# The order of gather and adding transfers in a mixture-of-experts loop

## The reference, cut to what matters

```python
logits = hf @ w_router + b_router
top_vals, top_idx = lax.top_k(logits, 4)
top_w = softmax(top_vals)
# for every block of rows that go to one expert e:
    xb  = hf[tok]                                              # gather
    hid = clamped_swiglu(xb @ w_gate_up[e] + b_gate_up[e])     # 1024 -> 2048 -> 1024
    out = (hid @ w_down[e] + b_down[e]) * wt[:, None]          # 1024 -> 1024
y = segment_sum(outs, row_tok)                                 # adding, four rows per token
x = rms_norm(x + gate2 * y)
```

## Time and profile before

| | |
|---|---|
| median of three runs | 2173.54 us |
| the profiled execution | 2171.81 us |
| its span | 2170.0 us |
| TensorE busy in the span | 2047.2 us, 94% |
| VectorE, ScalarE, GpSimd busy | 837.4, 264.7, 279.2 us |
| moved by DMA | 546.12 MB |
| TensorE matmuls of `gate_up` | 6336, which is 33 items of 192 |
| gathers | 34 |
| adding transfers | 99 |

### The profile page before, as it was taken

How to read it: one execution, slowest core, us unless ns; L and a number is a source line. 1 busy time by engine, 2 the same in 40 slices (tenths; PEclk the granted TensorE clock), 3 DMA queues, 4 the chain that set the end, 5 groups by cost and what they waited for, 6 DMA issues and landing times.

```text
span 2170.0 us, 42668 instructions
## 1 busy us (share of the span) xinstructions
PE 2047.2 (94%) x16720; PEld 984.2 (45%) x16720; DVE 837.4 (39%) x2052; ACT 264.7 (12%) x585; POOL 279.2 (13%) x290
## 2 busy tenths in 40 slices
PE   6999999999989999997999999999999999999995
PEld 3554665456544444445334344344443443434432
DVE  1567876687664000036323222232232322323223
ACT  2121212122222000001001000010010100101001
POOL 0011111111110000000021121211212112122122
PEclk9999999999999999996999999999999999999997
DMA  9323332333043223245899999999999999999994
GB/s 318 98 59 117 117 116 58 116 116 116 2 125 126 78 67 87 71 184 221 316 380 394 381 396 392 394 399 387 397 390 381 400 391 396 393 384 398 385 354 167
DMA packets 194563, 546.12 MB, mean 252 GB/s; under 512 B 18259, under 2 KB 133627, under 8 KB 141791
## 3 DMA queue, kind: packets, MB, share of 16 engines
q1 hardware_dynamic: 175272, 523.52, 64.3%
q0 software_dynamic: 18064, 21.80, 4.6%
q10 hardware_dynamic: 1191, 0.31, 0.1%
HBM read 530.79 MB, written 19.35 MB: 254 GB/s over the span
## 4 chain that ended last, share of the span: by engine, by line
PE 58%; DMA 20%; issue 9%; DVE 7%; POOL 5%; SPq 1%; DVEq 1%; ACT 1%; POOLq 0%; ACTq 0%
PE ps L1425 32%; DMA hT<-h_rows,tok 18%; PE ps L1776 16%; POOL acc_rows L616 5%; PE ps L1754 4%; DMA ring<-in_w_ada_dram 2%; DVE c L1020 2%; PE ps L1741 1%; DVE zs L1354 1%; PE ps L1545 1%; DVE ring L997 1%; PE ps L1502 0%; PE ps L1536 0%; PE ps L1548 0%; DMA yT<-acc_rows 0%
## 5 line engine op out<-in xcount | busy, mean ns | idle before, releaser
L1754 PE MATMUL ps<-ring,hT 128*32 128x512 f32 x6336 | 690.0, 595 | 1.1 <-ACT hT L873 1.1
L1425 PE MATMUL ps<-hT,ring 128*128 128x512 f32 x1008 | 443.0, 598 | 0.0
L1754 PEld LDWEIGHTS ps<-ring,hT 128*32 128x32 f32 x6336 | 203.5, 110 | 461.3 <-issue 457.5
L1776 PE MATMUL ps<-ring,seg 128*32 128x256 f32 x6336 | 348.7, 380 | 1.0 <-ACT seg L882 1.0
L1425 PEld LDWEIGHTS ps<-hT,ring 128*128 128x128 f32 x1008 | 192.3, 192 | 232.7 <-issue 232.1
L1305 DVE TENSOR_TENSOR hT<-ps,bgu 128x512 f32<-128x512 f32 x99 | 67.9, 686 | 543.7 <-PE ps L1754 543.7
L616 POOL DMA_INDIRECT acc_rows<-zs,scur x99 | 153.3, 1548 | 906.5 <-DVE zs L1354 858.0
L1776 PEld LDWEIGHTS ps<-ring,seg 128*32 128x32 f32 x6336 | 202.5, 110 | 135.2 <-ACT seg L882 1.2
L1020 DVE SCALAR_TENSOR_TENSOR c<-ring,pcur,c 128x512 f32<-128x512 f32 x232 | 155.5, 743 | 0.0
L865 ACT ACTIVATE mm<-hT 128x256 f32<-128x256 f32 x99 | 44.9, 454 | 767.9 <-DVE hT L1307 767.9
L1425 PE MATMUL ps<-yT,ring 128*128 128x512 f32 x256 | 111.2, 592 | 1.0 <-ACT yT L737 1.0
(11 more groups left out here) (270 smaller groups left out, 1418.5 us busy)
## 6 DMA issues: line engine op xcount, KB each, us to landing
ring<-in_w_gate_up_dram SPq DMA_DIRECT2D x264, 1024.0 KB, 15.2
ring<-in_w_down_dram SPq DMA_DIRECT2D x132, 1024.0 KB
ring<-in_w_ada_dram SPq DMA_DIRECT2D x24, 1024.0 KB, 8.8
ring<-in_w_in_dram SPq DMA_DIRECT2D x48, 512.0 KB, 4.2
ring<-in_w_in_dram SPq DMA_DIRECT2D x16, 1024.0 KB, 5.4
ring<-decay_rows SPq DMA_DIRECT2D x8, 1024.0 KB, 7.3
ring<-in_w_ssm_out_dram SPq DMA_DIRECT2D x8, 1024.0 KB, 5.5
yT<-in_x_dram SPq DMA_DIRECT2D x2, 2048.0 KB, 8.3
```

The costliest lines, as they stand in the source:

```text
L1425: last = T.matmul(out_, lhs(k), rhs(k), start=(k == 0), stop=(k == n - 1))
L1754: last = T.matmul(ps[j * GT:(j + 1) * GT, g, :], xT[:, k, g * GT:(g + 1) * GT], gu[:, k, j * GUW:(j + 1) * GUW], start=(k == 0), stop=(k = ...
L1776: last = T.matmul(ps[j * GT:(j + 1) * GT, 3 + g // 2, (g % 2) * DW:(g % 2 + 1) * DW], hidT[:, k % 2, g, k // 2, :], dn[:, k, j * DW:(j + 1 ...
```

## The change

Two orders change. On GpSimd, `gather(i)` used to stand ahead of `add_rows(i-2)`; now it stands ahead of `add_rows(i-3)`, so that the gather of item i+1 is issued ahead of the adding transfers of item i-2, where it used to be behind them. On VectorE, the copy of the token numbers moves from the start of an iteration (after the results of the iteration before) to the place between `swiglu(i)` and `results(i-1)`, and it copies the numbers of one item later. The loops' bounds follow: one gather more is issued in all, of a table column that is added for it (NTAB grows from 54 to 55). No wait is taken away or added.

```diff
-NTAB = MAXI + 1
+NTAB = MAXI + 2
...
-        eidf = xdecf[0:1, 384:384 + MAXI + 1]
+        eidf = xdecf[0:1, 384:384 + NTAB]
...
             gather(2)
+            gather(3)
             add_rows(0, first=True)
-            with pool.Fori(3, items + 1) as i:
+            with pool.Fori(4, items + 2) as i:
                 gather(i)
-                add_rows(i - 2)
+                add_rows(i - 3)
             add_rows(final)
...
             swiglu(1)
+            token(3)
             results(0, first=True)
             with dve.Fori(2, items) as i:
-                token(i + 1)
                 swiglu(i)
+                token(i + 2)
                 results(i - 1)
             results(final)
```

## The result

The changed kernel takes 2147.49 us (median of four runs, 2146.75 to 2149.30) against 2172.82 us of the kernel before (four runs, 2170.99 to 2175.83: the three known already and one more). The ratio is 0.9881, 95% interval 0.9865 to 0.9897. The profiled execution took 2146.75 us, its span is 2145.0.

What follows compares the result with a forecast made beforehand. TensorE and the DMA engines were taken to bind in turn, with a late gather in the loop: 2171.8 - 10.5 + 2 + 0.5 = 2163.8 us, 1.7 more for the median, so 2165, range 2151 to 2172.

Steps and rivals of the forecast that it cites:

- What bounds: Expert loop: TensorE and DMA both near their limits; waiting for the late gather costs 0.76 us per item.
- The gather leaves the loop: GpSimd: gather issued some 14.5 us earlier, so TensorE's wait of 0.76 us per item goes, -21.9 us.
- some 14 us before the adding transfers: Sign of being right, on GpSimd: how far the gather's issue would precede its iteration's adding transfers.
- What the moves put behind them: Adding transfers on GpSimd and results on VectorE now stand behind moved operations but go out as before: cost nothing.
- one column and one gather more: Wider token table costs +0.1 to +0.2 us, the extra gather after the last swiglu 0 to +1, taken as 0.3.
- The weight loads: Expert loop: load backlog grows 1.1 us per item until TensorE waits, giving back about half of the 21.9 us.
- each item takes 34.1: Slowest DMA engine's time per item, 33.72 + 0.37 us, setting the period once TensorE waits for loads, after 18.7 items.
- the ceiling: Gate and up loads: landing may take 30.2 us before TensorE waits for them.
- The term of sequence: Loop's end: a gather and adding transfers pass ahead of the last gate and up load, 0 to 4.3 us, taken as 2.
- the first one: Rival: TensorE alone binds the loop, the DMA catches up, the whole 21.9 us comes; median 2152 us, chance 0.16.
- The second rival: Weight loads take all back: a load may wait only some 20 us, period 34.1 at once; 2172 us, chance 0.17.
- The rules weighed: DMA limits from the skill, 435 GB/s fabric and about 358 from HBM, set against the trace's 393 and 423.

Runs made afterwards that it cites:

- held transfers: Changed kernel with the adding transfers held back one item and issued just ahead of the next gather, after its token numbers are copied: 2160.84 us, ratio 0.9932.
- more rows: Changed kernel with 96 rows of 4 KB more per item loaded on SyncE's queue to a place nobody reads: 2237.43 us, ratio 1.0281.

## Why the prediction was wrong

*What bounds.* Right: with the gather ahead of the adding transfers the wait is gone whether the copy is early or not, with the gather behind them it stays, and the period without it is 32.96 us.

*The gather leaves the loop.* Right in mechanism and size: -21.9 us counted, 21.9 measured between the two profiles. The part that I put on the earlier copy is not needed: the order on GpSimd alone gave it all, the copy alone nothing. One sign was misstated: I asked for the gather's issue "some 14 us before the adding transfers", but 14.5 us was the distance to its own old place. From the same rows it should have been 1527.91 - 1519 = 9 us; 8.0 were measured.

*What the moves put behind them, one column and one gather more.* Right, nothing of it can be seen.

*The weight loads.* This step failed, by the size of one term: "each item takes 34.1". I took period plus growth, read from one kernel, for a fixed amount of work that would stay when order and period changed. It was 33.7 us (33.5 with the order alone). With a growth of 0.73 in place of 1.12, my own sum reads (30.2 - 8.2) / 0.73 = 30 items, which is all of them, and the ceiling is reached as the loop ends: nothing is given back. The ceiling itself was right, as the runs with held transfers and with more rows show. Two things are in the 0.4 to 0.6 us of the error. With the gather ahead of the adding transfers an item costs 0.3 to 0.4 us less at the old period; with the gather behind, it costs 0.3 to 0.4 less when items follow faster. They don't add up: both together take away no more than the 0.4 to 0.6. Why an item costs less then isn't shown. The 34.1 itself was no misreading: with the gather behind, items bound by loads took 34.10 us. It held for an order that the change takes away.

*The term of sequence* (+2 us) belonged to a limit that didn't bind, and fell with it.

*The rivals.* The time is nearly that of the first one, 2152 against 2147.5 measured, but its mechanism didn't come true. It needed "a DMA that catches up", with landing times "that stay below 25 us to the end". The DMA didn't catch up: the landing time grew by 0.73 us per item, twice as fast as before, to a median of 28.5 us. TensorE alone bound the loop because there are only 33 items; that the loop ends just as the backlog comes to its ceiling is luck. A longer loop would meet the waits of the forecast, later and with a smaller price (an estimate from 33.7 against 32.96: 0.7 us per item). Its half about the order is wrong too: gather and adding transfers may be in flight together, the gather must only not lie behind. I gave it 0.16 and let the evenness of the old growth speak against it, which could only speak for the old order. Of the 4.6 us that its time lacks, 3.0 are the earlier start of item 2 and 0.5 the added column and gather, of which nothing is seen; 0.9 come from the 1.7 added for the median, where this profile lies 0.7 below its own.

The second rival counted on the gate bias, which lies behind the weights in the queue. VectorE did stand idle longer ahead of the operation that takes this bias in, 193.2 us in all between 1100 and 2120. The table of waits names no releaser; the program waits there for the load of the bias:

```profile
DVE bgu L1326 <- issue: 193.2, 24, 16.3
```

Its wait for the sums of `gate_up`, with the bias there in time, is 18.6 us at the longest, so the 16.3 left some 2 us, as counted, and nothing waited for VectorE in turn.

*The spread of the start.* No single profile of before could tell that item 2 may begin 6 us earlier or later from one execution to the next; the range had no room for it.

*The rules weighed.* The ceiling of about 358 GB/s for loads from HBM (the Trainium skill, DMA: Bandwidth & Descriptors, "Where 436 GB/s comes from") as what binds a load is contradicted a second time by 400 GB/s over 200 us. (The same page says, under the table "Measured (HBM→SBUF, 128 partitions, SWDGE, issued from GpSimd)", that a core gets about 358 when both cores of the HBM domain stream. Here one core runs, so with that condition trace and page don't disagree.) The ceiling of 435 on the same page isn't reached either: in the run with the added bytes over 128 partitions TensorE waited for loads while 13.7 MB moved per item of 34.65 us, an estimated 395 GB/s; the window table has 400 there.

## What to carry to other kernels

A load's landing time that grows from item to item says that the DMA engines are behind; but period plus growth is the cost of this order at this pace, not a constant. Before it is used against a gain, one run with the order changed and TensorE slowed to the old pace separates the two.

When transfers of two kinds share a queue, put the one that somebody waits for ahead, as here; the copy that feeds it need not be early, only early enough.

## What the runs showed of the hardware that was not expected

Beside the same weight loads, 96 rows of 4 KB over 96 partitions cost the DMA 3.1 to 3.6 us per item, the same 0.393 MB as 3 KB on each of 128 partitions about 1.0 (34.65 - 33.7). That the shape decides is shown; whether by the number of partitions or the length of a row, and by which engine or port, is not.

When the loads' landing time nears 28 us, the issue of a small load on SyncE's queue takes 4.67 us instead of 0.59, both in the changed kernel, the short one at 1502.94 and the long one at 2030.30 us:

```profile
1502.94 0.59 SPq L467 DMA_DIRECT2D yT<-in_b_gate_up_dram  x1
```

```profile
2030.30 4.67 SPq L467 DMA_DIRECT2D yT<-in_b_gate_up_dram  x1
```

As I read it, part of the backlog then stands in the issuing queue, and the landing time, counted from the issue, no longer shows all of it; no run here tests that.
